# Expert loop of a routed MLP: each iteration works off its two blocks to the end, instead of carrying the second block's down product into the next iteration

## The reference, cut to what matters

```
D_MODEL = 1024; N_GROUPS = 4; EXPERTS_PER_GROUP = 8; N_EXPERTS = 32; TOP_K = 2; EXPERT_HIDDEN = 512

def hier_moe(h, w_rg, b_rg, w_re, b_re, w_up, w_down):
    ...
    def expert_block(args):
        xb, e = args
        g, u = jnp.split(xb @ w_up[e], 2, axis=-1)
        return (jax.nn.silu(g) * u) @ w_down[e]

    y = lax.map(expert_block, (buf.reshape(n_blocks, MOE_BLOCK, D), blk_expert)).reshape(-1, D)
    y = y[dest] * gate.reshape(-1)[order][:, None].astype(h.dtype)
    return jax.ops.segment_sum(y, tok_sorted, num_segments=n_tok)
```

## Time and profile before

| | us |
|---|---|
| median of three runs | 2885.49 |
| lowest and highest run | 2878.11, 2891.11 |
| the profiled execution's own time | 2878.88 |
| its span (first to last instruction) | 2877.1 |
| PE busy in it | 2753.3 (96%) |
| PE busy between 2500 and 2700 us, in the expert loop | 200.00 of 200.00 |
| data moved in that stretch | 409 GB/s |
| phase of `experts`, from the first transposes of rows to the first work of `combine` | 2265.04 to 2831.12 |

### The profile page before, as it was taken

How to read it: one execution, slowest core, us unless ns; L and a number is a source line. 1 busy time by engine, 2 the same in 40 slices (tenths; PEclk the granted TensorE clock), 3 DMA queues, 4 the chain that set the end, 5 groups by cost and what they waited for, 6 DMA issues and landing times. The chain is left out here.

```text
span 2877.1 us, 44043 instructions
## 1 busy us (share of the span) xinstructions
PE 2753.3 (96%) x18251; PEld 1644.0 (57%) x18251; DVE 1505.0 (52%) x2099; ACT 776.8 (27%) x1444; POOL 66.4 (2%) x90
## 2 busy tenths in 40 slices
PE   8999899999999998999999998999999799999996
PEld 4444564444444443444454445657554699999994
DVE  7886676566666668774653007867674311111113
ACT  2111771111111114421200106757332212111211
POOL 0000000000000000000000000000000000000002
PEclk9999999999999999999999999999999899999998
DMA  3122851111111117763321000004200899999995
GB/s 139 35 74 37 258 185 68 49 44 44 44 44 44 44 50 258 268 251 127 77 59 66 30 0 12 1 1 120 97 12 10 331 400 409 408 408 409 409 366 186
DMA packets 80309, 422.64 MB, mean 147 GB/s; under 512 B 11200, under 2 KB 20928, under 8 KB 64192
## 3 DMA queue, kind: packets, MB, share of 16 engines
q1 hardware_dynamic: 58528, 362.29, 34.2%
q10 hardware_dynamic: 15664, 41.95, 4.0%
q0 software_dynamic: 6000, 16.78, 1.7%
HBM read 384.68 MB, written 51.38 MB: 152 GB/s over the span
## 5 line engine op out<-in xcount | busy, mean ns | idle before, releaser
L3572 PE MATMUL ex_up_ps<-big,ex_xT 128*32 128x128 f32 x3072 | 349.1, 274 | 0.0
L3570 PE MATMUL ex_up_ps<-big,ex_xT 128*32 128x384 f32 x3072 | 344.8, 490 | 0.7 <-ACT ex_xT L3657 0.6
L3572 PEld LDWEIGHTS ex_up_ps<-big,ex_xT 128*32 128x32 f32 x3072 | 334.3, 110 | 0.6
L2204 PE MATMUL dn_acc<-big,V 128*128 128x512 f32 x506 | 220.9, 597 | 13.9 <-PEq L45 11.5
L1754 PE MATMUL fm_ring<-h,V 128*128 128x512 f32 x504 | 219.7, 592 | 0.0
L295 DVE TENSOR_SCALAR_CACHE_REDUCE h<-ad_s_ps 128x1280 f32<-128x1280 f32 x64 | 92.9, 1489 | 172.7 <-PE ad_s_ps L204 172.7
L3572 PE MATMUL ex_y_ps<-ex_wd,ex_hT 128*32 128x128 f32 x1536 | 174.4, 274 | 0.0
L2204 PEld LDWEIGHTS dn_acc<-big,V 128*128 128x128 f32 x506 | 96.4, 191 | 136.1 <-issue 131.8
L3570 PE MATMUL ex_y_ps<-ex_wd,ex_hT 128*32 128x384 f32 x1536 | 172.3, 489 | 0.8 <-DVE ex_hT L3715 0.8
L3572 PEld LDWEIGHTS ex_y_ps<-ex_wd,ex_hT 128*32 128x32 f32 x1536 | 168.6, 111 | 0.4
L1754 PEld LDWEIGHTS fm_ring<-h,V 128*128 128x128 f32 x504 | 95.8, 190 | 120.5 <-issue 120.5
(11 more groups left out here) (594 smaller groups left out, 4775.1 us busy)
## 6 DMA issues: line engine op xcount, KB each, us to landing
big<-in_w_eup SPq DMA_DIRECT2D x64, 2048.0 KB
ex_wd<-in_w_edown SPq DMA_DIRECT2D x32, 2048.0 KB, 20.3
V<-in_w_down SPq DMA_DIRECT2D x35, 704.0 KB, 5.6
dn_tail<-in_w_mod ACTq DMA_DIRECT2D x48, 512.0 KB, 5.3
fm_up<-in_w_up SPq DMA_DIRECT2D x22, 1028.0 KB, 4.9
y_dram<-in_cos SPq DMA_DIRECT2D x1, 21504.0 KB, 72.9
y_dram<-big ACTq DMA_DIRECT2D x32, 288.0 KB
dn_tail<-in_w_in SPq DMA_DIRECT2D x17, 512.0 KB, 4.5
```

The costliest lines, as they stand in the source:

```text
L2204: mm = nc.tensor.matmul(down_bank(kind, m), weights[:, k * P:(k + 1) * P], src[:, k, :], start=(k == 0), stop=(k == KH - 1))
L3570: nc.tensor.matmul(o[32 * g:32 * g + 32, 0:W], rows(g), w[:, 0:W], start=first, stop=last)
L3572: mm = nc.tensor.matmul(o[BR:P, g * P:(g + 1) * P], rows(g), w[:, W:BANK], start=first and g == 0, stop=last and g == GR - 1)
```

## The change

On all engines the loop body becomes the pair as a whole. PE runs gate 0, up 0, gate 1, up 1, down 0, down 1, with the transposes of the second hidden block and of the next pair's first rows between the two down products. DVE, ACT and SP follow that order. The tail behind the loop is gone, and the loop ends at 27 (`PAIRS`) and not at 28, since 2048 assignments in blocks of 96 rows over 32 experts never need more than 54 blocks. SP loads the down weights of block 1 right at the start.

```
+PAIRS = 27
...
                 load_down(0, 0, 0)
-                with sp.Fori(1, NB // 2) as i:
+                load_down(0, 1, 1)
+                with sp.Fori(1, PAIRS) as i:
                     with sp.If(i * 2 < nb):
                         load_gate_up(i, 0)
-                        load_down(i - 1, 1, i * 2 - 1)
                         load_gate_up(i, 1)
                         load_down(i, 0, i * 2)
-                pairs = sp.value_load(r["count"][0:1, 1:2], min_val=1, max_val=NB // 2)
-                load_down(pairs - 1, 1, pairs * 2 - 1)
+                        load_down(i, 1, i * 2 + 1)
...
+                def pair(i, first=False):
+                    product(i, 0, 0, first)
+                    turn(i, 1)
+                    product(i, 0, 1)
+                    product(i, 1, 0)
+                    turn_hidden(i, 0)
+                    product(i, 1, 1)
+                    down(i, 0)
+                    turn_hidden(i, 1)
+                    turn(i + 1, 0)
+                    down(i, 1)
...
-                with pe.Fori(1, NB // 2) as i:
+                with pe.Fori(1, PAIRS) as i:
                     with pe.If(i * 2 < nb):
-
-                        product(i, 0, 0)
-                        turn_hidden(i - 1, 1)
-                        turn(i, 1)
-                        product(i, 0, 1)
-                        down(i - 1, 1)
-                        product(i, 1, 0)
-                        turn_hidden(i, 0)
-                        turn(i + 1, 0)
-                        product(i, 1, 1)
-                        down(i, 0)
-                pairs = pe.value_load(r["count"][0:1, 1:2], min_val=1, max_val=NB // 2)
-                turn_hidden(pairs - 1, 1)
-                down(pairs - 1, 1)
+                        pair(i)
...
+                def pair(i):
+                    silu(i, 0)
+                    keep_x(i, 1)
+                    silu(i, 1)
+                    store_y(i, 0)
+                    keep_x(i + 1, 0)
+                    store_y(i, 1)
...
-                        silu(i, 0)
-                        keep_x(i, 1)
-                        store_y(i - 1, 1)
-                        silu(i, 1)
-                        keep_x(i + 1, 0)
-                        store_y(i, 0)
...
+                def pair(i):
+                    multiply(i, 0)
+                    keep_hidden(i, 0)
+                    multiply(i, 1)
+                    keep_y(i, 0)
+                    keep_hidden(i, 1)
+                    keep_y(i, 1)
...
-                        keep_hidden(i - 1, 1)
-                        multiply(i, 0)
-                        keep_y(i - 1, 1)
-                        keep_hidden(i, 0)
-                        multiply(i, 1)
-                        keep_y(i, 0)
```

More of the change, by code:

```diff
@@ L3551, in _ @@
                 gather(1, 0, 1)
-                with pool.Fori(1, NB // 2) as i:
+                with pool.Fori(1, PAIRS) as i:
                     with pool.If(i * 2 < nb):
@@ L3618, in down @@
                     mm.then_inc(y_done, 1)
-                turn(0, 0)
[L3621 to L3628, removed]
+                def pair(i, first=False):
[9 more added lines that the diff above has]
+                    down(i, 1)
+                turn(0, 0)
+                pair(0, True)
                 nb = used(pe)
-                with pe.Fori(1, NB // 2) as i:
+                with pe.Fori(1, PAIRS) as i:
                     with pe.If(i * 2 < nb):
-                        product(i, 0, 0)
-                        turn_hidden(i - 1, 1)
-                        turn(i, 1)
-                        product(i, 0, 1)
-                        down(i - 1, 1)
-                        product(i, 1, 0)
-                        turn_hidden(i, 0)
-                        turn(i + 1, 0)
-                        product(i, 1, 1)
-                        down(i, 0)
-                pairs = pe.value_load(r["count"][0:1, 1:2], min_val=1, max_val=NB // 2)
-                turn_hidden(pairs - 1, 1)
-                down(pairs - 1, 1)
+                        pair(i)
             @block.scalar
@@ L3682, in _ @@
                 act.wait_ge(y_filled, 16)
[L3683 to L3687, removed]
+                def pair(i):
[5 more added lines that the diff above has]
+                    store_y(i, 1)
+                pair(0)
                 nb = used(act)
-                with act.Fori(1, NB // 2) as i:
+                with act.Fori(1, PAIRS) as i:
                     with act.If(i * 2 < nb):
-                        silu(i, 0)
-                        keep_x(i, 1)
-                        store_y(i - 1, 1)
-                        silu(i, 1)
-                        keep_x(i + 1, 0)
-                        store_y(i, 0)
+                        pair(i)
                 pairs = act.value_load(r["count"][0:1, 1:2], min_val=1, max_val=NB // 2)
-                store_y(pairs - 1, 1)
                 for u in range(2):
@@ L3731, in keep_y @@
                                             r["gate5"].rearrange(by_group, g=GR, c=2), ALU.mult).then_inc(y_kept, 1)
[L3733 to L3737, removed]
-                    with dve.If(i * 2 < nb):
-                        keep_hidden(i - 1, 1)
-                        multiply(i, 0)
-                        keep_y(i - 1, 1)
-                        keep_hidden(i, 0)
-                        multiply(i, 1)
-                        keep_y(i, 0)
-                pairs = dve.value_load(r["count"][0:1, 1:2], min_val=1, max_val=NB // 2)
-                keep_hidden(pairs - 1, 1)
-                keep_y(pairs - 1, 1)
+                def pair(i):
[5 more added lines that the diff above has]
+                    keep_y(i, 1)
+                pair(0)
+                with dve.Fori(1, PAIRS) as i:
+                    with dve.If(i * 2 < nb):
+                        pair(i)
                 dve.sem_inc(hid_ready, 1)
```

## The result

| | before | changed |
|---|---|---|
| median of 20 runs, us | 2885.28 | 2889.61 |
| lowest and highest | 2878.11, 2893.29 | 2883.09, 2898.82 |
| span of the profiled execution, us | 2877.1 | 2883.1 |
| first transposes of rows to first work of `combine`, us | 2265.04 to 2831.12: 566.08 | 2265.86 to 2836.76: 570.90 |

The ratio of the times is 1.0019, with a 95% interval of 1.0011 to 1.0027: the changed kernel is 0.19% slower, some 5.5 us (3.2 to 7.8). The difference is small but real, since the interval leaves out 1, on the side that was forecast and within the 0.5% that the forecast counted as no change. The median is also inside the forecast's own range of 2883 to 2907 us. In the two profiled executions the phase of `experts` is 4.8 us longer; it began 0.8 us later, and what comes behind it took 0.4 us more.

The account below looks back on a forecast made before the run. PE was taken to bound the kernel: +14.3 us of longer breaks in the loop and -6.2 us in the tail give +8.1 us on 2885.5, so 2893.6 us, with 2883 to 2907 as the range for 8 in 10.

Parts of the forecast that it names:

- PE sets the pace, and what is added to its stream is paid in full: Expert loop: PE waits for no transfer or engine, a pair takes 33.98 us, and additions are paid once per pair.
- The rival in which the transfers set the pace: Expert loop: longer breaks would be free and only the tail would count, 2879 us; chance 0.06.
- The wait between the down products: Between a pair's down products: keep_hidden runs behind keep_y on DVE, PE waits 0.70 us, break 2.03 us.
- 0.21 later: Between the down products: PE's next weight load follows the end of the copy to hT by 0.21 us.
- The 0.15 us for waking VectorE in the upper bound: Break between down products: 0.15 us more for waking DVE behind a wait that has only just come true.
- The rival with a pause between two VectorE operations: Between keep_y and keep_hidden: a pause of up to 0.96 us, adding up to 14.4 us, 2908 us; chance 0.12.
- The third break: In each pair of the loop: turn_hidden standing alone costs a break of 0.62 us, lower bound 0.32.
- The sum over the loop: Up to the end of down(15, 0): breaks total 56.5 us against 42.2, +14.3 us, bounds +9.5 to +18.1.
- The tail: From the end of down(15, 0) to the next phase: 16.6 us against 22.8, -6.2 us, between -6.8 and -4.6.
- the 1.5 us for the barrier: End of the experts phase: closing barrier taken as 1.5 us, between 0.92 and at most 3.1.
- The net: Whole kernel: loop +14.3 and tail -6.2 give +8.1 us, 2893.6 us, bounds +2.7 to +13.5.
- Buffers: Loop loads and ACT's copy: 8.5 and 2.3 us to spare, loads landing a little sooner; late-buffer rival 2908 us, chance 0.08.

Follow-up runs that it names:

- e7: Kernel before, but from pair 1 on turn() transposes one of eight pieces of a block's rows: 16.42 us a block for 11 blocks, then 16.97 for 15.
- e6: Kernel before, with loops ending at the number of pairs, loaded once ahead of the loop: median 2872.84 us against 2884.51, ratio 0.9964.
- e1: Changed kernel, with block 1's copy to hT on ScalarE instead of VectorE: break between down products 1.48 us against 1.88, phase 565.03 against 570.90.
- e2: Changed kernel, with VectorE making block 1's copy to hT ahead of block 0's keep_y: break 2.32 us against 1.88, phase 578.62 against 570.90.
- e3: Kernel before, with block 1's row transposes moved behind block 0's up product, three breaks a pair: pair 34.28 us against 33.99, phase 571.48 against 566.08.
- e4: Kernel before, with each engine's loop ending at the number of pairs, loaded ahead: tail 12.82 us against 22.76, phase 556.73 against 566.08.
- e5: Changed kernel, with each engine's loop ending at the number of pairs, loaded ahead: tail 12.39 us against 16.00, phase 568.04 against 570.90.

## Why the prediction was right

- **PE sets the pace, and what is added to its stream is paid in full.** This held: the period went up by 0.83 us and no wait for a transfer came up. It held by less than I thought. The rival in which the transfers set the pace, to which I gave 0.06, is wrong for this change, but e7 shows the two within some 0.03 us a block of each other once the buffers' lead is gone. A change that shortens PE's stream would have kept its gain only as long as that lead lasts, 11 blocks in e7.
- **The wait between the down products: mechanism right, size too large.** I put the break at 2.03 us, it is 1.88. The term "0.21 later" for PE behind the copy was read from the tail of before; in the loop it is 0.05. The lower clock of that tail isn't the reason, since e6 has 0.2 at the full clock. The rows of PE's sequencer show one: in the tail of before it still runs two instructions between the copy's end at 2818.80 and the load at 2819.01, and in the changed loop the semaphore instruction is over at 2334.63, before the copy ends at 2335.01, and nothing is left in between. First the two of before, then the one of the changed kernel:

```profile
L3609 PEldq FUSED_REGOPS  x1: 37/37/37, 2818.8 to 2818.8; - x1
L3611 PEldq EVENT_SEMAPHORE  x1: 51/51/51, 2818.9 to 2818.9; - x1
...
L3611 PEldq EVENT_SEMAPHORE  x1: 51/51/51, 2334.6 to 2334.6; - x1
```

`keep_hidden` starts 0.88 us behind `keep_y`'s start and not 0.96, as the earlier trace rows hinted. The start of `keep_y` was 0.40 behind the product instead of 0.30: the 0.30 was that of pair 0, and the 31 other blocks of the kernel before have 0.40. Together -0.15 a pair. That the last two nearly cancel is luck. The 0.15 us for waking VectorE in the upper bound came from no row, and no run shows it: the copy follows `keep_y` without idle time. e1 and e2 show by intervention that it is VectorE's order and both single buffers. A second buffer for `hT` or `y_ps`, the direct remedy, was not tried.
- **The rival with a pause between two VectorE operations** (0.12) is refuted: none is seen. The Trainium skill's "VectorE: DVE Perf Modes", section "The DRAIN you can't avoid", speaks of a flush ahead of the next operation, but adds that an operation that is not held starts earlier, which the prediction left out. The trace agrees with that addition: here the next one starts 0.08 us before the reported end of the one ahead.
- **The third break.** 0.62 us for a lone `turn_hidden` is 0.67; I had left out that its last load is followed by 0.17 and not by 0.11. e3 gives 0.29 us a pair in the period for a split alone, 0.06 us less than the sum of the breaks. The changed kernel's period shows the same 0.06: its breaks add 0.90 us and the pair 0.83. The six products between the breaks take that much less, and why isn't resolved.
- **The sum over the loop** was to be +14.3 us up to the end of `down(15, 0)`. It is 2820.76 - 2265.86 = 554.90 against 2808.36 - 2265.04 = 543.32, so +11.6. This is the term that was mis-sized, by the points above: -0.15 x 15 for the new break, +0.05 x 16 for the lone `turn_hidden`, -0.06 a pair for the rest that isn't resolved, and -0.2 for breaks that are 1.337 and not 1.33.
- **The tail** was to give 6.2 us and gives 6.8 (16.00 against the 16.6 forecast). ACT was through 15.1 us behind `down(15, 0)`, as forecast; what was too large is the 1.5 us for the barrier, which took 0.9, the lower bound. e4 confirms the part of before, empty iterations of PE with the clock's fall, and e5 that empty iterations held the end of after.
- **The net** was to be +8.1 us and is +4.8 in the phase of the profiles and +5.5 (3.2 to 7.8) by the ratio.
- **Buffers.** No late one was seen, as forecast. Landing times were not "a little sooner": the median went from 20.3 to 11.5 us, and e5, with the same loop, shows 10.7. The prediction had the direction and missed the size, since it didn't see how near the queue was to its limit (see e7).

## What to carry to other kernels

Two products of the same kind that share a single buffer on either side are best kept one other product apart: side by side, the evictions of the first and the input copy of the second add up on whichever engine has both. A loop with a fixed end and a test inside costs 0.45 to 0.75 us for each iteration that does nothing, and it matters where that falls: ahead of the last work it is paid in full and takes the clock with it, behind it only in part. Look at what a reordering does to such a tail apart from what it does to the steady state; here the tail gave back 6.8 of the 11.6 us that the loop lost, and the better kernel takes one from each side.

## What the runs showed of the hardware

- A whole stage can stand at the balance of PE and transfers without a wait on either side: at 409 GB/s and a DMA share of 1.01 PE had no gap, and with PE 0.57 us a block faster (e7) the gain lasted 11 blocks and was then gone, at 412 GB/s.
- PE's weight load follows 0.05 us behind the copy it waits for when nothing else is left to do (the loop of the changed kernel), 0.12 us behind `keep_y` in e1 and e2, and 0.21 us where its sequencer has a register and a semaphore instruction in between (the tails of before, e4 and e6), at the lower clock and at the full one alike.
- Where PE and the transfers are nearly balanced, the time from issue to landing tells the slack: 20 us at 33.99 us a pair, 11 us at 34.83, and up to 28.8 in e7.
- `combine`, which the edits leave alone, took 46.0 us in one profile and 49.7 in another, by its gathers' landing. A single whole time can hide or fake an effect of 5 us in the loop; the loop's own stretch can't.
